# Stacking the input rows of a state-space stage: SBUF-to-SBUF transfers in place of TensorE matmuls with pieces of the identity

## What is computed

```python
bu_re = jnp.einsum('bsgc,gpc->bsgp', u, bb_re)
bu_im = jnp.einsum('bsgc,gpc->bsgp', u, bb_im)
...
_, _, h_re, h_im = lax.associative_scan(
    _complex_affine_combine, (a_re_t, a_im_t, bu_re, bu_im), axis=1)
y = (jnp.einsum('bsgp,gcp->bsgc', h_re, c_re)
     - jnp.einsum('bsgp,gcp->bsgc', h_im, c_im)
     + d_skip * u)
```

## Time and profile before

| | |
|---|---|
| runs | 810.74, 810.84, 813.1 us; median 810.84 |
| the profiled execution | 809.15 us |
| its span | 807.1 us |
| TensorE busy | 744.8 us, 92% |
| VectorE busy | 595.7 us, 74% |
| ScalarE busy | 389.5 us, 48% |
| GpSimd busy | 208.2 us, 26% |
| chain that ended last | TensorE 64%, VectorE 19%, issue 8%, ScalarE 6%, DMA 2% |

### The profile page before, as it was taken

One profiled execution on the slowest core, in us unless ns is written; L12 is line 12 of the kernel. 1 busy time (PEld: TensorE's weight loads), 2 busy tenths in 40 slices (PEclk: granted clock), 3 DMA queues, 4 the chain that ended last, 5 costly groups with the idle time before them and its releaser, 6 DMA issues.

```text
span 807.1 us, 17682 instructions
## 1 busy us (share of the span) xinstructions
PE 744.8 (92%) x6676; PEld 669.7 (83%) x6676; DVE 595.7 (74%) x935; ACT 389.5 (48%) x651; POOL 208.2 (26%) x121
## 2 busy tenths in 40 slices
PE   4589999999899999999999888998999999999996
PEld 0176999667788989898989778997979999999994
DVE  7854555895778888888898886677557776676675
ACT  2254544555464444454444543334456555555554
POOL 5900000121315445544544234552000000000000
PEclk9789999999989999999999989999989999999998
DMA  8869655496726777777765311111644556555531
GB/s 313 345 224 369 215 182 182 184 411 262 266 79 249 251 258 258 260 260 256 256 247 175 134 53 54 54 54 62 201 131 131 184 182 198 168 180 192 171 102 53
DMA packets 45979, 157.51 MB, mean 195 GB/s; under 512 B 6257, under 2 KB 7793, under 8 KB 45937
## 3 DMA queue, kind: packets, MB, share of 16 engines
q1 hardware_dynamic: 43632, 148.55, 52.6%
q10 hardware_dynamic: 1728, 6.29, 2.0%
q0 software_dynamic: 576, 2.10, 0.7%
HBM read 155.87 MB, written 1.05 MB: 194 GB/s over the span
## 4 chain that ended last, share of the span: by engine, by line
PE 64%; DVE 19%; issue 8%; ACT 6%; DMA 2%; POOL 1%; DVEq 0%; ACTq 0%; POOLq 0%
PE up L326 11%; PE up L328 11%; PE up L327 11%; PE acc L326 7%; DVE wlo L978 7%; PE acc L327 7%; PE acc L328 7%; ACT whi L719 3%; PE gv L362 2%; DVE ffn L1232 2%; DMA ffn<-in_mw 1%; DVE hl L1007 1%; DVE diag L999 1%; PE up L667 1%; PE acc L642 1%
## 5 line engine op out<-in xcount | busy, mean ns | idle before, releaser
L978 DVE TENSOR_TENSOR wlo<-raw,whi 128x1024 fp32r<-128x1024 f32 x194 | 304.5, 1586 | 102.0 <-ACT whi L719 100.8
L326 PE MATMUL up<-hh,whi 128*128 128x256 f32 x944 | 272.0, 288 | 4.3 <-DVE hl L1007 3.0
L327 PE MATMUL up<-hl,whi 128*128 128x256 f32 x944 | 269.3, 285 | 0.0
L328 PE MATMUL up<-hh,wlo 128*128 128x256 f32 x944 | 269.2, 285 | 0.0
L719 ACT ACTIVATE whi<-raw 128x1024 fp32r<-128x1024 f32 x194 | 200.9, 1051 | 35.3 <-PE acc L328 24.4
L326 PEld LDWEIGHTS up<-hh,whi 128*128 128x128 f32 x944 | 183.5, 194 | 16.1 <-issue 11.1
L327 PEld LDWEIGHTS up<-hl,whi 128*128 128x128 f32 x944 | 183.7, 195 | 0.0
L328 PEld LDWEIGHTS up<-hh,wlo 128*128 128x128 f32 x944 | 183.4, 194 | 0.0
L326 PE MATMUL acc<-ah,whi 128*128 128x256 f32 x352 | 100.4, 285 | 6.8 <-DVE wlo L978 6.6
L327 PE MATMUL acc<-al,whi 128*128 128x256 f32 x352 | 99.6, 283 | 0.0
L328 PE MATMUL acc<-ah,wlo 128*128 128x256 f32 x352 | 99.5, 283 | 0.0
(11 more groups left out here) (200 smaller groups left out, 915.5 us busy)
## 6 DMA issues: line engine op xcount, KB each, us to landing
raw<-in_w SPq DMA_DIRECT2D x194, 512.0 KB, 3.5
mraw<-in_mw SPq DMA_DIRECT2D x60, 512.0 KB, 6.3
arena<-in_mw SPq DMA_DIRECT2D x12, 512.0 KB, 11.6
tmp<-in_mw SPq DMA_DIRECT2D x6, 512.0 KB, 7.9
ffn<-in_mw SPq DMA_DIRECT2D x6, 512.0 KB, 8.6
tmp<-in_mw ACTq DMA_DIRECT2D x4, 512.0 KB, 7.5
ffn<-in_mw ACTq DMA_DIRECT2D x4, 512.0 KB, 9.6
mraw<-in_mw ACTq DMA_DIRECT2D x4, 512.0 KB, 14.3
```

Of the source, the lines that this page charges most:

```text
L326: pe.matmul(out, w_h, xh, start=first, stop=False, skip_group_check=skip)
L327: pe.matmul(out, w_h, xl, start=False, stop=False, skip_group_check=skip)
L328: return pe.matmul(out, w_l, xh, start=False, stop=last, skip_group_check=skip)
L978: dve.tensor_tensor(wlo[:, n % SPL, :], raw[:, n % RAW, :], whi[:, n % SPL, :].bitcast(F32), ALU.subtract).then_inc(lo_ready, 1)
```

## The change

`u` is stored by place in the chunk first: (m, l, j) instead of (m, j, l), so that u[:, m, l, :] is 64 neighbouring numbers; ScalarE's copy writes it in that order. `y` in `up` has the same order; L and E address it so, and `skip` reads both so and writes `yv` in token order. S is gone from TensorE, with ScalarE's copy of its result and the semaphores `st_done` and `st_ready`. In its place sixteen DMA transfers per tile, each 32 partitions by 64 numbers (8 KB), copy pieces of u straight to `ust`: twelve (l = 0, 1, 2) are issued by SP, four (l = 3) by ScalarE after its copy to bpow. `inject` waits for all sixteen by one semaphore for each buffer of `ust`. SP's weight loads stand between the stacks of transfers: those up to slot W_SIN + 8 before the first, then one behind each.

```diff
-        u = ffn[:].rearrange("p (m j l) -> p m j l", m=KT, l=LCH)
+        u = ffn[:].rearrange("p (m l j) -> p m l j", m=KT, l=LCH)
...
-            for n in range(W_SIN, W_SIN + 3):
+            def stack_u(mt):
+
+                sp_.wait_ge(u_ready, mt + 1)
+                if mt >= 2:
+                    sp_.wait_ge(v_done, mt - 1)
+                for l in range(LCH - 1):
+                    for q in range(4):
+                        sp_.dma_start(ust[32 * l:32 * l + 32, mt % 2, q, :],
+                                      u[32 * q:32 * q + 32, mt, l, :]).then_inc(stacked[mt % 2], 16)
+
+            for n in range(W_SIN, W_SIN + KT + 1):
                 load_w(n)
-            first = W_SIN + 3
+            for mt in range(KT):
+                stack_u(mt)
+                load_w(W_SIN + KT + 1 + mt)
+            first = W_SIN + 2 * KT + 1
...
-            def stack_u(mt):
-
-                pe.wait_ge(u_ready, mt + 1)
-                for q in range(4):
-                    for l in range(LCH):
-                        mm = pe.matmul(acc[32 * l:32 * l + 32, mt % 2, T + q * NJ:T + (q + 1) * NJ],
-                                       ident[:, 32 * q:32 * q + 32], u[:, mt, :, l], start=True, stop=True)
-                mm.then_inc(st_done, 1)
...
-                pe.wait_ge(st_ready, mt + 1)
+                pe.wait_ge(stacked[mt % 2], 16 * 16 * (mt // 2 + 1))
...
-                y = up[:, mt % 2, 0:T].rearrange("p (j l) -> p j l", l=LCH)
+                y = up[:, mt % 2, 0:T].rearrange("p (l j) -> p l j", l=LCH)
                 for lag in range(LCH):
-                    pe.matmul(y[:, :, lag:LCH], kbd[:, mt, lag, :], u[:, mt, :, 0:LCH - lag],
+                    pe.matmul(y[:, lag:LCH, :], kbd[:, mt, lag, :], u[:, mt, 0:LCH - lag, :],
                               start=(lag == 0), stop=False, skip_group_check=True)
...
-                            mm = pe.matmul(y[32 * q:32 * q + 32, :, l], cpow[:, (l + 1) % 4, r, pair * 32:pair * 32 + 32],
+                            mm = pe.matmul(y[32 * q:32 * q + 32, l, :], cpow[:, (l + 1) % 4, r, pair * 32:pair * 32 + 32],
...
-                    act.activation(ffn[:, m * T:(m + 1) * T], acc[:, m % 2, 0:T], ACT.Copy).then_inc(u_ready, 1)
+                    act.activation(u[:, m, :, :].rearrange("p l j -> p j l"),
+                                   acc[:, m % 2, 0:T].rearrange("p (j l) -> p j l", l=LCH), ACT.Copy).then_inc(u_ready, 1)
...
-                    act.wait_ge(st_done, m + 1)
+                    act.wait_ge(u_ready, m + 1)
                     if m >= 2:
                         act.wait_ge(v_done, m - 1)
-                    act.activation(ust[:, m % 2, :, :].rearrange("p q j -> p (q j)"), acc[:, m % 2, T:2 * T],
-                                   ACT.Copy).then_inc(st_ready, 1)
+                    for q in range(4):
+                        act.dma_start(ust[96:128, m % 2, q, :], u[32 * q:32 * q + 32, m, 3, :]).then_inc(stacked[m % 2], 16)
...
-                dve.scalar_tensor_tensor(yv[:, mt % 2, :], ffn[:, mt * T:(mt + 1) * T], dcol[:, mt:mt + 1],
-                                         up[:, mt % 2, 0:T], ALU.mult, ALU.add).then_inc(yv_ready, 1)
+                by_l = "p (l j) -> p l j"
+                dve.scalar_tensor_tensor(yv[:, mt % 2, :].rearrange("p (j l) -> p l j", l=LCH), u[:, mt, :, :],
+                                         dcol[:, mt:mt + 1], up[:, mt % 2, 0:T].rearrange(by_l, l=LCH),
+                                         ALU.mult, ALU.add).then_inc(yv_ready, 1)
```

More of the change, by code:

```diff
@@ L235, in build @@
         kz = sem("kz")
-        st_done, st_ready = sem("st_done"), sem("st_ready")
+        stacked = [sem(f"stacked{a}") for a in range(2)]
         tab_arg, tab_ready = sem("tab_arg"), sem("tab_ready")
@@ L675, in _ @@
                     if m >= 2:
-                        pe.wait_ge(st_ready, m - 1)
+                        pe.wait_ge(u_ready, m - 1)
                     if m == 0:
@@ L685, in _ @@
                 if m == KT:
-                    pe.wait_ge(st_ready, KT)
+                    pe.wait_ge(u_ready, KT)
                 if m >= KT:
@@ L691, in _ @@
                     emit(m - 2)
-                if m < KT:
-                    stack_u(m)
             for m in range(KT):
```

## The result

The changed kernel takes 818.92 us in the median of four runs (818.15 to 821.44), the kernel before 811.02 beside it. The ratio is 1.0104 (1.0084 to 1.0123): about 8 us slower. I had forecast 810.1, no change, and had given the range from 807.0 to 816.0 eight chances in ten: the result lies above it.

A forecast was written before the change was run, and what follows sets the result against it. TensorE's work was taken to bound the state-space stage's 8.90 us intervals, with GpSimd 0.45 us behind. Steady part -2.4, start +0.8 and end +0.9 sum to -0.7 us: 810.1 against 810.84, eight-in-ten range 807.0 to 816.0.

The forecast's parts named there:

- What a transfer costs: Stack transfers: 0.47 us from one to the next (0.37 to 0.6), 1.9 to land; twelve on SP land after 7.1 us.
- Steady part: Four intervals, tile 3 to 7: TensorE loses S (0.93 us) but waits for GpSimd; 8.2 us each, -2.4 in all.
- Start: Start of the state-space stage: first inject waits for the stack and runs at half clock, E at full clock; +0.8 us.
- End: End of the stage: the last inject waits for the stack, perhaps at half clock, and ends late; +0.9 us.
- Priced at nothing: ScalarE's four issues, later weight loads, stepped writes in skip and copy (up to 0.4 us more each, about 0.8 in all): 0.
- The order of y: E and L matmuls write y whole instead of with a step of four: no gain, times kept.
- the transfers take the place of the removed wait: Rival, 35%: stack transfers cost about what the removed wait saved, slower or near it; with shared issuing +4.6 us, 815.4.
- far end: Part of that rival, 5 of its 35%: above 0.65 us per issue SP alone exceeds 8.4 us per interval; +8 and more.
- issues shared between SP and ScalarE: Part of that rival: both engines share the forming of transfers, so sixteen go out in 7.5 us; total +4.6, 815.4.

The follow-up runs named there:

- the run with rows from HBM: Changed kernel, its sixteen transfers per tile each reading a weight tile in HBM instead of u: 813.31 us against 811.83 beside it, ratio 1.0029.
- GpSimd cut short: Changed kernel without any stacking, GpSimd's last two instructions per tile cut to 8 of 63 chunks: 804.97 us, ratio 0.9917.
- Five issues with twice the way: Changed kernel, but SP writes each tile of u to HBM in one transfer and reads it back stacked in four: 810.83 us, ratio 0.9993.
- the run with four forms: Changed kernel with four SP transfers per tile instead of sixteen, by tile from u or HBM with 32 or 128 rows: 810.20 us, ratio 0.9981.

## Why the prediction was wrong

**The step that failed** is "What a transfer costs": 0.47 us from one to the next, with 0.6 as the upper end. It measured 0.63, outside both ends. I took it from loads and stores, each of which has one side in HBM, and looked at rows and bytes for a reason to go lower; what raised it is that both sides are in SBUF, since with the source alone put into HBM the issue took 0.42. The long issue of 0.5 to 0.9 us more in most groups I had not thought of at all. The 0.16 us between 0.63 and 0.47 enters twelve times before the first inject, twelve times per interval and twelve times before the last inject.

Point by point:

1. Steady part. Sum -2.4, measured +0.1. The mechanism was right: without a stack GpSimd holds TensorE at 8.24 us an interval (8.2 in the sum), and with cheap issues at 8.35. But SP with 8.8 to 9.1 us of issues per interval came above both. I had written that above 0.65 us per issue SP alone would pass 8.4 us; with the long issue counted that point lay between 0.57 and 0.61.
2. Start. Sum +0.8, measured +3.7. Twelve issues and the landing took 475.80 to 485.0, 9.2 us for 7.1. TensorE's half clock in the first inject came as expected, 3.65 us for 3.5. So did the gain of a full clock in the first E (1.10 us long for 1.84). With issues at 0.46 the start was +1.0.
3. End. Sum +0.9, measured +5.3. VectorE's timeline after shows the last two turn_ins:

```profile
541.88 0.69 DVE L1321 TENSOR_TENSOR tmp<-acc,arena 128x512 f32<-128x512 f32 x1 [0.28 <-PE acc L646]
...
552.52 0.69 DVE L1321 TENSOR_TENSOR tmp<-acc,arena 128x512 f32<-128x512 f32 x1 [3.76 <-PE acc L646]
```

   The last turn_in begins 14.5 us after the last P (538.03) instead of 9.94; I had 11.0. SP was busy with tile 6 and its weight load until 539.2, half a microsecond after u of tile 7 was ready, then took 8.2 us, and the inject ran at half clock. The second error is the clock behind the last inject. In the run with rows from HBM the last turn_in begins 11.4 us after the last P, close to my 11.0, but the end is 24.38 us instead of 22.4. TensorE's timeline there, last inject and L:

```profile
542.51 2.77 PE L646 MATMUL acc<-tmp,arena 128*128 128x64 f32 x16 [3.35 <-DMA tmp<-in_w]
545.08 2.55 PE L658 MATMUL up<-ffn,mraw 128*128 128x256 f32 x8
```

   L takes 2.55 us where it took 1.43 before, at a granted clock of 0.50 from 545 to 548 us, and the GLU matmuls behind it begin at half clock too; the chain that ended last runs through all of them. My sum let the slow stretch end with inject. The same L took 2.55 us after the change. From the start of the last turn_in to the end of the last GELU it is 13.0 us there, 12.4 after the change and 11.6 before. This is read from the traces; no run tests it by itself. A third point is open: without a stack the end is 1.7 us longer in the new order (23.19 against 21.48), which I had put at nothing. Of that 1.3 us lie ahead of the last turn_in, which with transfers waits for inject anyway, so it cannot simply be added.
4. "Priced at nothing". The copy of u and skip took 0.24 and 0.20 us more, inside the 0.4 that I allowed. But I priced them at 0.8 us in all; the stages of the two runs without stacking differ by 2.0 us, in ratio 0.3%, at the edge of the noise. How the steps come to cost that is not shown: with GpSimd cut short they cost the intervals nothing. No wait for a weight load appears after the change, and without ScalarE's four issues the time was no lower; to that extent the rest of this part held.
5. The order of y. Right: no gain from it, 220 and 222 ns in E and, without stacking, the same 326 ns for the 192-column lag in both orders. The sentence of the Trainium skill (SBUF — State Buffer, Door 1: The DMA port swizzle, its note on cachelines) that any non-contiguous PSUM access slows matmuls much is not what these runs show. What the same note says of SBUF, that a line is 16 bytes and each access to a new line costs, does agree with S: reading u with a step of 16 bytes it took 1.11 us, whole rows 0.63.

Of the rivals, "the transfers take the place of the removed wait" happened, at its far end, to which I gave 5 of its 35%. That end named SP alone, above 0.65 us per issue, and this is what came, at 0.63 with the long issues on top. The rest of the rival, issues shared between SP and ScalarE, did not: the pitch was 0.63 with ScalarE silent. That a surprise would rather be a loss was foreseeable from the sum itself, since the gain it could bring at best was small. A free stack gives 0.4%.

## What to carry to other kernels

Before moving small work from an engine to transfers, count their issues on one queue: here a transfer of 8 KB cost its issuer 0.6 us, so sixteen cost more than the 0.93 us of matmuls that they replaced. Five issues with twice the way beat sixteen direct ones by 8 us. Where an engine waits at the head and tail of a pipeline, the full latency counts, and TensorE can pay the wait twice, once more in its clock, and not only in the matmuls right behind the wait. And before removing an operation, ask whether its operands only lie badly: storing u so that TensorE reads whole rows took S from 1.11 to 0.63 us and, with y in its old order, gave a kernel 0.3% faster than the one before and 1.3% faster than the change.

## What the runs showed of the hardware

- Issuing on SP: 0.59 us with source and destination in SBUF, 0.42 to 0.44 from HBM, back to back; the first of most groups 0.51 and, SBUF to HBM and alone, 0.34. Rows (32 or 128) made no difference. SP's weight loads, from HBM, took 0.58 right behind SBUF-to-SBUF issues, 0.33 to 0.43 in the runs with transfers from HBM.
- In most groups of twelve issues one took 0.5 to 0.9 us longer (505.73, 1.47 us), often some 4.5 us behind a 512 KB load, but not in every group (495.08), and in the run with four forms one came 6.5 us behind.
- After a TensorE wait of 1.59 us came a stretch of more than 6 us at 1.2 GHz, after one of 1.36 us more than 3; waits of 0.77, 0.98, 1.39 and 1.72 were followed by none.
- With a step of 16 bytes in the moving operand (the one that streams through TensorE) S took 1.11 us, without 0.63; the same step in the PSUM output of E cost nothing (222 and 220 ns). ScalarE's copy of 256 columns: 0.63 us when it writes with a step, 0.39 when it reads PSUM with one. VectorE's skip: 0.66 with a step in either the source or the destination, 0.46 with none.
